# Where DVE sums two of an even job's three cache pages beside gated linear attention

## The chip, the cores and the metric

One core of a Trainium2 chip runs the whole program. The metric is the device time of one execution in microseconds. Engines: PE (TensorE, with PEld for its weight loads), DVE (VectorE), ACT (ScalarE), POOL (GpSimd) and SP (SyncE, which only issues DMAs here). Each engine runs its own instructions strictly in the order in which they are written; engines meet through counting semaphores (`S("name")`).

## What is computed

One inference step of a small hybrid decoder: a gated-linear-attention (GLA) layer, then a stick-breaking attention layer over a shared, paged K/V cache, for 512 prompt tokens and for 8 sample tokens with 2048 cached positions each. What matters here:

```
# GLA, per head h of 4, in 8 chunks of 64 tokens
o_intra = tril(q_in @ k_in^T) @ v
S_c     = decay_c * S_(c-1) + k_dec_c^T @ v_c        # state steps, chunk by chunk
o       = o_intra + q_in @ S_(c-1)
out     = (rms_norm(o) * silu(g)) @ w_out             # g = hn @ w_in[:, gates]

# scores of the 8 samples against the cache: 8 x 16 pages of 128 keys, 16 heads of 64
z[page, key, head] = sum_d k_cache[page, key, head, d] * q[sample, head, d]
```

The scores of the cache don't depend on the prompt's GLA. They are spread over the long run of matrix products as filler for POOL, DVE and ACT.

## The kernel before, in words

**Jobs.** The prompt's matrix products are cut in jobs of 128 output columns (`PHASES`, L38): gk 0 and 1, q 2 to 5, k 6 to 9, v 10 to 17, g 18 to 25, wo0 26 to 33, ple0 34 to 41, q1 42 to 49, g1 50 to 57 and so on. A job up to g uses three products of split weights (`product`, L1727): ACT makes the high part of the weights (`split_hi`, L736), DVE the low part (`split_lo`, L1210 to L1216), and PE waits for it by `w_split`. Jobs of wo0, ple0, q1 and g1 are unsplit (L1744, L1747).

**The page pipeline.** The cache's keys come as 128 pages of 512 KB. For page n: SP loads it in a slot (`load_page`, L533 to L542); POOL, or for some pages DVE (L1401), multiplies it by the sample's query (`multiply_pages`, L634 to L642); then DVE sums over each head's 64 features (`score_pages`, L1389 to L1403, the TENSOR_REDUCE of L1402), or ACT for some pages with 16 activations (`sum_page`, L900 to L909). `PAGES_AT` (L66 to L74) deals pages to jobs, and job j sums the pages dealt to job j-1: in phase g three a job. With `FEW` = 32, pages 0 to 31 turn round in four slots (L84 to L94) and later ones in eight, so in phase g page n is loaded when page n-4 has been summed (`slot_free`, L498 to L512, semaphore `k_used`). SP issues in order: pages, the rows of queries (L544 to L550), and ahead of page 36 `w_up0`, which waits for the last attention output (`o_mm`) and the last store of states (`st_out`, L563 to L567). From page 32 on the first page of each job is summed by ACT (`ACT_SUMS`), in wo0 to ple0. Page n+8 then waits for it.

**Phase g on PE** (L2041 to L2053 and L1984 to L2039). Job 18+u is a gate product; u//2 is the head h. An even u is followed by `gla_turned(h-2)` (transposes, L2037), `gla_output(h-1)` (L2022, L2026), which waits for all 8 state steps of head h-1, and `gla_scores(h)` (transposes L1995, products L2003), which from h = 2 waits for `gated`, that is for `gate_o(h-2)` on DVE. An odd u is followed by `gla_states(h)` (L2015), the products that the state steps take in. After job 25 come products of wo0 mixed with `gla_turned(2)`, `gla_output(3)` and `gla_turned(3)` (L2061 to L2077).

**Phase g on DVE** (L1463 to L1490). The order is written out by hand. Each job: `gate_normed` (L1453) on the product; an odd job then has the 8 state steps of its head (`state_steps`, L1435 and L1438), an even one `gate_o(h-2)` (L1447); then `gate_silu` (L1459), which waits for ACT's sigmoid; an even job also the masked copy of the scores (L1481). `state_steps(h)` of a head after the first waits until the previous head's final state has been stored from the same tile (`st_out`; the store is ACT's, L928) and its outputs are done (`o_mm`). `score_pages(job, part, parts)` sums a part of a job's pages. With three pages, (0, 2) is the first page and (1, 2) the other two. The calls before the change:

- an odd job u (up to 5), at its end: the first page of its three
- the next even job, between norm and silu: the other two pages of the odd job
- an even job, at its end: all three of its pages (two in job 18)

**Phase g on ACT** (L946 to L973): high splits, sigmoid of the gate (L788), for an even job the store of the state, the sum of squares and copies of the output (`o_copies`, L926 to L934), the copy of the keys (L970) and the norm of the output (`o_rms`, L936 to L944).

**wo0.** On DVE each job adds the residual (`add_residual`, L1497) and sums pages; on ACT (L996 to L1007) each job asks for weights, sums its first page, and then copies and squares the residual tile (`x_hi`, L747, and L761). The first product of ple0 takes in those eight tiles.

Of the kernel before, what the change touches and what calls it, by code (L numbers as in the profile page):

```python
# [152 lines left out]
def pages_at(job):  # L153
    return range(PAGES_THROUGH.get(job - 1, 0), PAGES_THROUGH.get(job, NPAGES))
# [17 lines left out]
def on_pool(n):  # L172

    return all(n - pages_at(j)[0] < pool_share(j) for j in PAGES_THROUGH if n in pages_at(j))


def pool_pages(n):

    return sum(on_pool(i) for i in range(n))


def on_act(n):

    return any(n in pages_at(j)[:ACT_SUMS.get(j, 0)] for j in PAGES_THROUGH)
# [11 lines left out]
def banks_of(j):  # L196

    m = tiles_through(j) - 1
    if wide(j):
        return (2 * (m % 2), 2 * (m % 2) + 1)  # L200
    return (m % 4,) if m >= FOUR_BANKS else (m % 2,)
# [31 lines left out]
def build(nc, x_prompt, x_sample, state_gla, cache_k, cache_v, page_table, p_prompt, p_sample,  # L233
# [3 lines left out]
    with ExitStack() as ctx:  # L237
# [179 lines left out]
        def S(name):  # L417
            if name not in sems:
                sems[name] = ctx.enter_context(nc.semaphore(name))
            return sems[name]  # L420
# [166 lines left out]
        def _(pool):  # L587
# [90 lines left out]
            def cut_causal(h):  # L678

                A = psig[h % 2]  # L680
                for e, (_, _, blocks) in enumerate(ZBANKS):
                    pool.wait_ge(S("sig_p"), h * len(ZBANKS) + e + 1)
                    if len(blocks) == 2:
                        own_blocks = A[:, 2 * P:4 * P].rearrange("p (b n) -> p b n", n=P)
                        pattern = [[0, 2], [-1, P]]
                    else:
                        c = PSEG[blocks[0]] + blocks[0] * P
                        own_blocks, pattern = A[:, c:c + P], [[-1, P]]
                    ins = nc.gpsimd.affine_select(out=own_blocks, in_=own_blocks, compare_op=ALU.is_ge, fill=0.0, base=-1,
                                                  pattern=pattern, channel_multiplier=1)  # L690
                ins.then_inc(S("sig_cut"), 1)
# [515 lines left out]
        def _(dve):  # L1207
            own = Steps(dve, S("dve_steps"))

            def split_lo(j):  # L1210

                if j >= NJOBS or unsplit(j):
                    return
                dve.wait_ge(S("w_hi"), splits_through(j))
                raw, hi, lo = split_views(j)
                nc.vector.tensor_tensor(lo, raw, hi.bitcast(F32), ALU.subtract).then_inc(S("w_split"), 1)  # L1216
# [172 lines left out]
            def score_pages(job, part=0, parts=1):  # L1389

                pages = pages_at(job - 1)
                for n in pages[len(pages) * part // parts:len(pages) * (part + 1) // parts]:
                    if on_act(n):
                        continue
                    at, b = slot[SLOT_OF[NSB + n]][:], n // NPG
                    if on_pool(n):
                        dve.wait_ge(S("k_mul_pool"), pool_pages(n + 1))
                    else:
                        dve.wait_ge(S(f"qb_in{b % 2}"), 16 * (b // 2 + 1))
                        dve.wait_ge(S(f"slot_in{SLOT_OF[NSB + n]}"), 16 * SLOT_TURN[NSB + n])  # L1400
                        own.then(nc.vector.tensor_tensor(at, at, qb[:, b % 2, :], ALU.mult))  # L1401
                    nc.vector.tensor_reduce(zall[:, n % NPG, b * SH:(b + 1) * SH], at.rearrange("p (h d) -> p h d", d=HD),  # L1402
                                            AX.X, ALU.add).then_inc(S("k_used"), 1)  # L1403

            for u in range(1, 8):
                j = PHASES["v"][0] + u
# [18 lines left out]
            def state_steps(h, chunks):  # L1425

                if h and chunks[0] == 0:
                    dve.wait_ge(S("st_out"), 16 * h)
                    dve.wait_ge(S("o_mm"), h)
                for c in chunks:  # L1430
                    kv = chunk_bank(c)
                    if c % 4 == 0:
                        dve.wait_ge(S("kv_mm"), h * NCH + c + 4)
                    if c == 0:
                        ins = nc.vector.tensor_copy(states[:, 0, :], kv)  # L1435
                    else:
                        dve.wait_ge(S("st_step"), h * NCH + c)
                        ins = nc.vector.scalar_tensor_tensor(states[:, c, :], states[:, c - 1, :],  # L1438
                                                             dec[:, h, c:c + 1], kv, ALU.mult, ALU.add)
                    ins.then_inc(S("st_step"), 1)  # L1440

            def gate_o(h):

                dve.wait_ge(S("o_t"), h + 1)
                for vt in range(2):
                    g = gT[:, 2 * h + vt, :]
                    last = nc.vector.tensor_tensor(g, bank[(4 if h < GH - 1 else 6) + vt], g, ALU.mult)  # L1447
                last.then_inc(S("gated"), 1)

            def gate_normed(j):  # L1450

                src, like = product_of(j)
                nc.vector.tensor_tensor(src, src, like(rstd[:]), ALU.mult).then_inc(S("g_n"), 1)  # L1453

            def gate_silu(j, u):

                src = bank[banks_of(j)[0]]
                dve.wait_ge(S("sigm"), u + 1)
                nc.vector.tensor_tensor(gT[:, u, :], src, work[:, 2 + u % 2, 0:NP_TOK], ALU.mult).then_inc(S("evac"), 1)  # L1459
# [3 lines left out]
            for u in range(8):  # L1463
                h = u // 2
                j = PHASES["g"][0] + u
                if u % 2 == 0 and u:
                    split_lo(j + 1)
                gate_normed(j)
                if u % 2:
                    state_steps(h, range(NCH))  # L1470
                    gate_silu(j, u)
                    if h < GH - 1:
                        score_pages(j, 0, 2)
                else:
                    if h >= 2:
                        gate_o(h - 2)
                    if h:
                        score_pages(j - 1, 1, 2)
                    gate_silu(j, u)
                    dve.wait_ge(S("att_mm"), h + 1)  # L1480
                    nc.vector.copy_predicated(attT[:, h % 2, :].rearrange("p (b n) -> p b n", b=TB), attm,  # L1481
                                              bank[5].rearrange("p (b n) -> p b n", b=TB)).then_inc(S("att_out"), 1)
                    split_lo(j + 2)
                    score_pages(j)

            score_pages(PHASES["g"][0] + 7, 0, 2)
            gate_o(GH - 2)
# [34 lines left out]
            for u in range(8):  # L1522
                j = PHASES["wo0"][0] + u
# [3 lines left out]
            for u in range(8):  # L1527
                j = PHASES["ple0"][0] + u
# [7 lines left out]
            for u in range(8):  # L1536
                j = PHASES["q1"][0] + u
# [27 lines left out]
            for i in range(24):  # L1565
                u = i % 8
                j = PHASES["g1"][0] + i
# [85 lines left out]
            for u in range(8):  # L1653
                j = PHASES["wo1"][0] + u
# [13 lines left out]
            for u in range(8):  # L1668
                j = PHASES["ple1"][0] + u
# [22 lines left out]
        def _(pe):  # L1692
# [34 lines left out]
            def product(j, x0, wait_x=False, tiles=range(KT)):  # L1727
# [8 lines left out]
                if unsplit(j):  # L1736
# [12 lines left out]
                    if tiles[-1] == KT - 1:  # L1749
                        last.then_inc(S("mm"), 1)  # L1750
                    return
                _, wh, wl = split_views(j)
                for k in range(KT):
                    if wait_x:
# [383 lines left out]
            def scores(h):  # L2138

                i = h // 2  # L2140
                if h == 0:
                    pe.wait_ge(S("evac"), last_tile("V"))
                pe.wait_ge(S("q_low"), h + 1)
                pe.wait_ge(S("qz_zero"), min(h + 1, 4))
                for e, (bk, _, blocks) in enumerate(ZBANKS):
                    if bk == SHARED and h >= 2:
                        pe.wait_ge(S("at_shared"), h - 1)
                    if h:
                        pe.wait_ge(S("sig_p"), (h - 1) * len(ZBANKS) + e + 1)
                    for q in blocks:  # L2150
                        c0, n = ZB[q][1], (q + 1) * P
                        for low in range(2):
                            last = nc.tensor.matmul(bank[bk][:, c0:c0 + n], qz[h % 4][:, low, q * P:(q + 1) * P],
                                                    (KE, KO)[h % 2][:, i, 0:n], start=(low == 0), stop=(low == 1),
                                                    skip_group_check=True)
                    last.then_inc(S("z_p"), 1)
# [149 lines left out]
```

## Time and profile before

| what | value |
|---|---|
| median of 3 runs | 868.82 us (868.79 to 869.54) |
| the profiled execution, its own time | 872.96 us |
| its span, first to last instruction | 871.2 us |
| PE busy | 818.4 us (94%) |
| DVE busy | 563.7 us (65%) |
| ACT busy | 480.7 us (55%) |
| POOL busy | 344.9 us (40%) |
| DMA | 236.79 MB, mean 272 GB/s |
| mean granted TensorE clock | 0.992 |

The span is that of one profiled execution; the times of the runs are taken without a profile. Phase g takes some 165 to 241 us of the span, wo0 some 243 to 318, ple0 and q1 from there to 437, and g1 follows. In a timeline, the number ahead of a bracket is the duration, and the bracket tells how long the engine was idle before that instruction and what ended the idle time ("issue": nothing that the profile shows). PE's products show two records for each matmul in 32-bit floats.

### The profile page before, as it was taken

The page shows a single profiled execution, that of the slowest core. Times are in us where ns is not written, and L with a number is a line of the kernel's source. Part 1 is how long each engine was busy: PE and PEld are TensorE (multiplying, and loading weights), DVE is VectorE, ACT ScalarE, POOL GpSimd, SP SyncE. Part 2 cuts the span into 40 slices and gives each one's busy share as a digit, 9 for nine tenths or more (in the row PEclk, how much of TensorE's full clock was granted, in tenths as well). Part 3 has the DMA queues.
Part 4 walks back from the last instruction along what each step waited for, and adds up shares of the span by engine and source line. Part 5 has one row for each costly group of instructions (what it writes and reads, how often), then busy time and mean ns, then how long its engine had stood idle before and what let it go on. Part 6 is the DMA issues. An engine that isn't in the chain of part 4 may idle for free.

```text
span 871.2 us, 14850 instructions
## 1 busy us (share of the span) xinstructions
PE 818.4 (94%) x5001; PEld 572.5 (66%) x5001; DVE 563.7 (65%) x620; ACT 480.7 (55%) x1603; POOL 344.9 (40%) x211
## 2 busy tenths in 40 slices
PE   5999999998999999999999999999969998999995
PEld 3666667876754434444488878777745454899995
DVE  4545375798966677878997744331179996655553
ACT  4611382335666677769886433412288895444433
POOL 3000000866685997885894000000266663011110
PEclk9999999999999999999999999999999999999998
DMA  9999868655689997997997099998888989521202
GB/s 330 380 368 340 315 221 297 209 187 212 206 283 378 385 344 250 328 350 262 392 392 272 1 351 335 361 331 290 314 317 299 341 332 370 184 97 49 98 1 99
DMA packets 109820, 236.79 MB, mean 272 GB/s; under 512 B 7505, under 2 KB 66712, under 8 KB 109488
## 3 DMA queue, kind: packets, MB, share of 16 engines
q1 hardware_dynamic: 51136, 174.29, 54.8%
q10 hardware_dynamic: 58608, 61.54, 21.0%
q8 instruction: 40, 0.66, 0.3%
q14 instruction: 36, 0.29, 0.1%
HBM read 222.54 MB, written 13.27 MB: 271 GB/s over the span
## 4 chain that ended last, share of the span: by engine, by line
PE 61%; DMA 12%; DVE 10%; ACT 8%; issue 3%; POOL 3%; SPq 2%; ACTq 0%; DVEq 0%; POOLq 0%
PE ps L1760 17%; PE ps L1747 13%; PE ps L1763 8%; PE ps L2197 5%; PE ps L1744 4%; DMA slot<-in_cache_k_dram 4%; PE ps L1724 2%; DMA work<-in_cache_v_dram 2%; DMA slot<-in_cache_v_dram 2%; POOL slot L641 2%; DVE w_lo L1216 2%; DMA w_raw<-in_gla_w_in_dram 2%; ACT slot L907 2%; DVE states L1438 2%; DVE zall L1402 1%
## 5 line engine op out<-in xcount | busy, mean ns | idle before, releaser
L641 POOL TENSOR_TENSOR slot<-slot,qb 128x1024 f32<-128x1024 f32 x97 | 249.2, 2600 | 100.2 <-DMA slot<-in_cache_k_dram 62.8
L1402 DVE TENSOR_REDUCE zall<-slot 128x16 f32<-128x1024 f32 x97 | 116.9, 1215 | 25.3 <-POOL slot L641 24.2
L1216 DVE TENSOR_TENSOR w_lo<-w_raw,w_hi 128x1024 fp32r<-128x1024 f32 x57 | 80.9, 1419 | 80.1 <-ACT w_hi L736 80.0
L907 ACT ACTIVATE slot<-slot 128x64 f32<-128x64 f32 x496 | 118.6, 241 | 18.4 <-POOL slot L641 18.3
L736 ACT CAST w_hi<-w_raw 128x1024 fp32r<-128x1024 f32 x58 | 60.6, 1045 | 72.1 <-PE ps L1763 36.3
L907 ACT ACTIVATION_READ_ACCUMULATOR slot<-slot 128x1 f32 x496 | 92.9, 187 | 0.0
L1747 PE MATMUL ps<-xn,w_raw 128*128 128x512 f32 x192 | 85.1, 595 | 1.3 <-ACT xn L747 1.3
L1747 PE MATMUL ps<-xn,w_unsplit 128*128 128x512 f32 x192 | 83.7, 593 | 0.0
L1763 PE MATMUL ps<-xa_hi,w_hi 128*128 128x512 f32 x200 | 81.7, 409 | 0.1
L1760 PE MATMUL ps<-xb_hi,w_hi 128*128 128x260 f32 x384 | 78.9, 287 | 1.1 <-DVE w_lo L1216 0.9
L1763 PE MATMUL ps<-xa_hi,w_lo 128*128 128x512 f32 x200 | 79.1, 396 | 0.0
L1763 PE MATMUL ps<-xa_lo,w_hi 128*128 128x512 f32 x200 | 78.7, 393 | 0.0
L1760 PE MATMUL ps<-xb_lo,w_hi 128*128 128x260 f32 x384 | 77.1, 282 | 0.0
L1760 PE MATMUL ps<-xb_hi,w_lo 128*128 128x260 f32 x368 | 74.0, 282 | 0.0
L2197 PE MATMUL ps<-slot,zs 128*32 128x512 f32 x480 | 63.1, 609 | 7.7 <-DMA work<-in_cache_v_dram 3.2
L1747 PEld LDWEIGHTS ps<-xn,w_unsplit 128*128 128x128 f32 x192 | 36.3, 190 | 46.2 <-issue 46.2
L1747 PEld LDWEIGHTS ps<-xn,w_raw 128*128 128x128 f32 x192 | 35.8, 190 | 46.6 <-issue 44.2
L1239 DVE TENSOR_TENSOR work<-ps,rstd 128x520 f32<-128x520 f32 (+1 forms) x40 | 27.7, 694 | 58.7 <-PE ps L1760 37.6
L1401 DVE TENSOR_TENSOR slot<-slot,qb 128x1024 f32<-128x1024 f32 x31 | 61.2, 1973 | 0.0
L1760 PEld LDWEIGHTS ps<-xb_hi,w_hi 128*128 128x128 f32 x384 | 59.0, 189 | 2.5 <-DVE w_lo L1216 1.1
L1760 PEld LDWEIGHTS ps<-xb_lo,w_hi 128*128 128x128 f32 x384 | 59.1, 188 | 0.0
L1760 PEld LDWEIGHTS ps<-xb_hi,w_lo 128*128 128x128 f32 x368 | 56.7, 188 | 0.0
(326 smaller groups left out, 1506.3 us busy)
## 6 DMA issues: line engine op xcount, KB each, us to landing
slot<-in_cache_k_dram SPq DMA_DIRECT2D x128, 512.0 KB, 6.2
slot<-in_cache_v_dram SPq DMA_DIRECT2D x120, 512.0 KB, 5.8
w_raw<-in_gla_w_in_dram ACTq DMA_DIRECT2D x12, 1024.0 KB, 6.6
slot<-in_gla_w_in_dram SPq DMA_DIRECT2D x24, 512.0 KB, 9.2
w_raw<-in_w_kv_dram ACTq DMA_DIRECT2D x8, 1024.0 KB, 11.0
w_raw<-in_w_ple_gate_dram ACTq DMA_DIRECT2D x6, 1024.0 KB, 5.5
s<-in_state_gla_dram SPq DMA_DIRECT2D x1, 4096.0 KB, 22.4
out_dram<-s ACTq DMA_DIRECT2D x4, 1024.0 KB, 8.2
```

What stands on the lines that cost most here:

```text
L641: nc.gpsimd.tensor_tensor(slot[s][:], slot[s][:], qb[:, (n // NPG) % 2, :], ALU.mult).then_inc(S("k_mul_pool"), 1)
L736: nc.scalar.copy(hi, raw).then_inc(S("w_hi"), 1)
L907: ins = nc.scalar.activation(part, part, ACT.Copy, accum_out=zall[:, n % NPG, b * SH + h:b * SH + h + 1])
L1216: nc.vector.tensor_tensor(lo, raw, hi.bitcast(F32), ALU.subtract).then_inc(S("w_split"), 1)
L1239: nc.vector.tensor_tensor(like(dst), src, like(rstd[:]), ALU.mult).then_inc(S("evac"), 1)
L1401: own.then(nc.vector.tensor_tensor(at, at, qb[:, b % 2, :], ALU.mult))
L1402: nc.vector.tensor_reduce(zall[:, n % NPG, b * SH:(b + 1) * SH], at.rearrange("p (h d) -> p h d", d=HD), AX.X, ALU.add).then_inc(S("k_used ...
L1744: last = nc.tensor.matmul(pp[m % 2][:, t, 0:H2], w[:, k, :], x[:, t * H2:(t + 1) * H2], start=(k == 0), stop=(k == KT - 1))
L1747: last = nc.tensor.matmul(bank[banks_of(j)[0]], w[:, k, :], x[:, 0:NP_TOK], start=(k == 0), stop=(k == KT - 1))
L1760: last = nc.tensor.matmul(pp[m % 2][:, t, 0:H2], w[:, k, :], x[:, t * H2:(t + 1) * H2], start=(k == 0 and first), stop=(k == KT - 1 and w ...
L1763: last = nc.tensor.matmul(bank[banks_of(j)[0]], w[:, k, :], x[:, 0:NP_TOK], start=(k == 0 and first), stop=(k == KT - 1 and w is wl))
L2197: last = nc.tensor.matmul(pp[3][32 * g:32 * g + 32, t, :], zs[:, c:c + 32], slot[SLOT_OF[e0 + g]][:, t * 512:(t + 1) * 512], start=(j0 == ...
```

## The change

On an odd job of phase g the two later pages of the even job before it are summed, in one more call behind the state steps and the gate; the even job sums at its end only the first page (one of its two pages in job 18, one of three in 20, 22 and 24). The order of pages stays 0, 1, 2 and so on. Nothing else differs: PE, ACT, POOL and SP have the same instructions.

```diff
                 if u % 2:
                     state_steps(h, range(NCH))
                     gate_silu(j, u)
+                    score_pages(j - 1, 1, 2)
                     if h < GH - 1:
                         score_pages(j, 0, 2)
                 else:
...
                     nc.vector.copy_predicated(attT[:, h % 2, :].rearrange("p (b n) -> p b n", b=TB), attm,
                                               bank[5].rearrange("p (b n) -> p b n", b=TB)).then_inc(S("att_out"), 1)
                     split_lo(j + 2)
-                    score_pages(j)
+                    score_pages(j, 0, 2)
 
             score_pages(PHASES["g"][0] + 7, 0, 2)
             gate_o(GH - 2)
```

## Rows read from the trace of the kernel before

**Rows 1.** The page, chain that ended last, share of the span by engine
```profile
PE 61%; DMA 12%; DVE 10%; ACT 8%; issue 3%; POOL 3%; SPq 2%; ACTq 0%; DVEq 0%; POOLq 0%
```

**Rows 2.** Windows: us, busy us (and count) by engine, clock, DMA share, GB/s
```profile
176.00:241.00 65.00, 58.87 (x317) 45.14 (x316) 58.02 (x70) 33.57 (x71) 43.16 (x19) 1.00 0.59 197
260.00:265.00 5.00, 5.00 (x19) 2.73 (x18) 0.46 (x1) 0.00 (x0) 5.00 (x3) 1.00 0.87 306
265.00:270.00 5.00, 4.49 (x11) 1.81 (x10) 1.52 (x3) 1.89 (x3) 2.42 (x2) 1.00 1.02 411
262.00:318.00 56.00, 54.71 (x139) 23.75 (x138) 40.65 (x35) 38.42 (x244) 45.84 (x19) 1.00 1.03 383
318.00:472.00 154.00, 154.00 (x470) 82.33 (x471) 129.94 (x112) 121.30 (x809) 121.06 (x46) 1.00 0.91 327
```

**Rows 3.** Timeline of PE: start us, us, line, operation, tiles, [idle before it <-releaser]
```profile
186.70 1.99 PE L2022 MATMUL ps<-vtok,attT 128*128 128x256 f32 x8 [1.01 <-DVE states L1438]
...
207.34 0.41 PE L2037 MATMUL ps<-ident,qT 128*128 128x128 f32 x2 [2.00 <-DVE states L1438]
...
213.64 0.63 PE L1995 MATMUL ps<-ident,kT 128*128 128x128 f32 x4 [1.64 <-issue]
...
234.31 0.63 PE L1995 MATMUL ps<-ident,kT 128*128 128x128 f32 x4 [1.37 <-issue]
...
247.59 0.41 PE L2037 MATMUL ps<-ident,qT 128*128 128x128 f32 x2 [0.54 <-DVE states L1438]
...
317.87 1.13 PE L1747 MATMUL ps<-xn,w_raw 128*128 128x512 f32 x2 [0.78 <-ACT xn L747]
```

**Rows 4.** Timeline of DVE, same columns
```profile
201.37 1.22 DVE L1402 TENSOR_REDUCE zall<-slot 128x16 f32<-128x1024 f32 x1 [3.40 <-POOL slot L641]
...
216.94 1.22 DVE L1216 TENSOR_TENSOR w_lo<-w_raw,w_hi 128x1024 fp32r<-128x1024 f32 x1
...
221.98 1.22 DVE L1402 TENSOR_REDUCE zall<-slot 128x16 f32<-128x1024 f32 x1 [1.56 <-POOL slot L641]
...
224.16 3.65 DVE L1438 SCALAR_TENSOR_TENSOR states<-states,dec,ps 128x256 f32<-128x256 f32 x7
...
229.45 2.96 DVE L1216 TENSOR_TENSOR w_lo<-w_raw,w_hi 128x1024 fp32r<-128x1024 f32 x1
...
232.93 1.27 DVE L1447 TENSOR_TENSOR gT<-ps,gT 128x512 f32<-128x512 f32 x2
```

**Rows 5.** The chain in order of time: start us, us, what
```profile
313.27 3.93 ACT slot L907 x32
```

**Rows 6.** All page sums of DVE in 176 to 260: duration ns min/median/max
```profile
L1402 DVE TENSOR_REDUCE zall<-slot x26: 1202/1211/1226, 179.7 to 258.4; 128x16 f32<-128x1024 f32 x26
```

**Rows 7.** Timeline of POOL, same columns
```profile
219.56 11.77 POOL L641 TENSOR_TENSOR slot<-slot,qb 128x1024 f32<-128x1024 f32 x5 [4.59 <-DMA slot<-in_cache_k_dram]
...
282.10 6.98 POOL L641 TENSOR_TENSOR slot<-slot,qb 128x1024 f32<-128x1024 f32 x3 [7.25 <-DMA slot<-in_cache_k_dram]
...
289.41 41.99 POOL L641 TENSOR_TENSOR slot<-slot,qb 128x1024 f32<-128x1024 f32 x16 [0.33 <-DMA slot<-in_cache_k_dram]
```

**Rows 8.** DMA issues, median us to landing: 196 to 236, 185 to 200, 274 to 300
```profile
slot<-in_cache_k_dram SPq DMA_DIRECT2D x11, 512.0 KB, 4.4
...
out_dram<-states ACTq DMA_DIRECT2D x1, 128.0 KB, 7.9
...
slot<-in_cache_k_dram SPq DMA_DIRECT2D x15, 512.0 KB, 7.6
```

**Rows 9.** Page 48: load, time to landing, and multiplication (second of the two)
```profile
L542 SPq DMA_DIRECT2D slot<-in_cache_k_dram x1: 338/338/338, 288.6 to 288.6; - x1
...
DMA to landing us min/median/max: 6.8/6.8/6.8
...
L641 POOL TENSOR_TENSOR slot<-slot,qb x2: 2367/2368/2368, 295.0 to 297.3; 128x1024 f32<-128x1024 f32 x2
```

## The prediction, made before the changed kernel was run

> **What bounds the kernel now.** I read the chain of waits first: TensorE (PE) carries 61% of it, DMA, DVE and ACT most of the rest [rows 1]. Then the stages [rows 2]. In the linear-attention stretch, 176 to 241 us, PE is not full and the DMA engines are little more than half busy. From 262 to 318 PE has 54.71 of 56 us and the DMA share is 1.03. From 318 to 472 PE is busy for all of 154 us, so what PE has gained at 318 it keeps there.
>
> PE's timeline has five stalls in the stretch [rows 3]: 1.01, 2.00 and 0.54 us for the state steps (L1438), and 1.64 and 1.37 us ahead of L1995, put down to "issue". The code tells those two: gla_scores waits for gate_o, whose L1447 ends on DVE at 234.20 [rows 4], just before PE goes on at 234.31. Together 6.56 us, the most that a quicker attention can give. At 317.87 PE waits 0.78 us for ACT's last copy of a residual tile [rows 3], which stands behind an ACT page sum that began as POOL's multiplication ended [rows 5], and that goes back to a page load. So the page pipeline and PE finish this stage together: a gain of PE alone buys nothing there.
>
> **What is late on DVE.** Before odd job 23, DVE idles 1.56 us for POOL's third page, sums it at 221.98, only then norms, and does the state steps from 224.16 (the copy before them from 223.7) to 227.8 [rows 4]. The change puts one sum there and two behind the gate. Seven sums move (one of two in job 18, two of three in 20, 22 and 24); none is added, none changes its engine, and the order of pages on DVE stays, so every counted wait keeps its meaning. A sum lasts 1.21 us [rows 6], and 1.12 us from start to start.
>
> **Part by part**, pair by pair:
> - Job 19: one sum less ahead, so norm and steps come 1.12 us earlier and the stall of 1.01 us goes. DVE has no less work and meets job 20 about when it does now, but page 11 is loaded 5 us later, so POOL should be idle at split_lo(21). A low split takes 1.22 us beside an idle POOL (216.94), 2.96 us when a multiplication is running (229.45: it ends 1.08 us after POOL's, at 231.33) [rows 4, 7]. I take 1 us of help.
> - Job 21: before it three sums and 3.40 us of waiting [rows 4] become one sum: norm at about 198.0 (now 202.5). A new wait comes: the steps write over states, and the previous head's store (ACT, about 190.7) takes 7.9 us to land [rows 8]. So steps start at about 198.6 and end at 202.7 (now 207.2). PE wants them at 207.34-2.00-1.01 = 204.3: the 2.00 us stall goes. Behind the steps come silu, three sums (to 206.7), split_lo(23), norm, and gate_o(0) at 209.7. PE is there at 213.64-1.64-3.01 = 209.0 and waits 0.8 instead of 1.64. Gained so far: 3.85.
> - Job 23: steps end near 223.1 (now 227.8). PE is at the next scores at 234.31-1.37-3.85 = 229.1, so at L2037 4.66 us before (as 212.00 follows 207.34), 224.4: no stall. gate_o(1) at 230.0: about 1.0 us. Gained: 4.2.
> - Job 25: PE's product ends at about 237.1, DVE is there first; steps end at 242.3. PE wants them at 247.59-0.54-4.2 = 242.85: no stall. Sum: **4.7 us** at the last L2037. Bounds: 3.6 if both gate_o stalls stay whole (1.01+2.00+0.54), 6.56 if all five go.
>
> Behind the two moved sums stand DVE's next low split, norm and gate_o. Their cover is the time won before them; if POOL is late they hold the gate_o that PE waits for.
>
> **The page ring.** In this stretch there are four slots: page n is loaded once page n-4 is summed. A load lands in 4.4 us (median), POOL takes 2.35 (11.77/5) [rows 7, 8]. The moved sums hold back loads 11, 16, 17, 20 and 21 by 2 to 6 us. Page 16: load at 204.6, multiplied by 211.5, wanted by DVE at 210.8, a wait of 0.7. Followed page by page, the later ones are wanted about when ready, since jobs 22 to 25 come earlier too. Pages 28 to 31 then run back to back on POOL, and page 31 is summed at 259.6, where it is now. So the ring costs nothing by its end and wins nothing: pages 32 to 39, the w_up load and the query rows on SP's queue stay. SP is held by those sums alone; its other work here is behind them and not due.
>
> **The next stage takes part of it back.** Load 40 waits for ACT's sum of page 32, which waits for PE's first residual tile, so it moves by 4.7 us. POOL now idles 7.25 us before page 40 [rows 7], room for that. But the DMA share is 1.03 [rows 2], page loads take 7.6 us [rows 8], and the same bytes must move in less time. Lower bound: no page lands earlier than now. Page 48 lands at 295.4 and is multiplied at 297.3 [rows 9]; POOL runs without a gap from 289.41 [rows 7], so its chain, ACT's sum and PE's 317.87 can still come 1.9 us earlier. Upper: all 4.7. Two 1 MB weight loads asked for 4.7 us sooner meet a share of 0.87 in 260 to 265 [rows 2] and fill 0.7 us of it. And 383 GB/s over the stage against 411 in its best 5 us leaves up to 56*(1-383/411) = 3.8 us. The DMA row, full, is what this stage is nearest to, so I stay in the lower half: 1.9+0.7, and 0.6 for the rate, **3.2 us**. PE then has 1.5 us of new stall before 318. Nothing later moves: PE has no gap to 472, and the page sums up to there follow it.
>
> Sum on the profiled execution: 872.96 (its span of 871.2 and 1.8 around it) becomes 869.8. The runs' median is 868.82, 4.1 below it; the same step gives 865.6. 0.2%, 1.74 us, is about what a measurement can tell from no change.
>
> **Two rules weighed.** The 26 sums take 1.202 to 1.226 us, POOL busy or not [rows 6]. The Trainium skill (Advanced Engine Details and Errata, VectorE Performance Modes) says that the second Vector SBUF port is shared with GpSimd and that the two then block each other. By that, if the sums used that port too, each would wait for POOL like the low split, and the moved ones would cost gate_o over 1 us each; the rows deny it for the sums. Second, the stage from 262 to 318 moved 383 GB/s [rows 2]. The skill (DMA: Bandwidth & Descriptors, Specifications) gives about 358 GB/s of HBM for a core. By that the stage had no room and the third case below would be the forecast; the measured rate is above it already.
>
> **Rivals.**
> - All of it passes (gain 4.7 to 6.6, 864.1): page loads land as early as they are asked for. For it: page 48 has 1.9 us in hand, and the rate has been 411. Against: share 1.03.
> - The page stage swallows it (gain 0 to 1.7, 868.3): the attention gains, but weights asked for earlier delay pages 36 to 40, POOL's gapless run starts no sooner and PE waits some 4 us at the end of the stage. For it: the tie at 317.87 and the share. Against: POOL's 7.25 us idle, and the 1.9.
> - Slower, by the page ring: each moved sum returns its slot late. With landings of 8.9 us (4.4 twice over), page 16 is ready 4.5 us later, DVE waits for it ahead of silu(22), and the delay goes round every fourth page. It decides once page 38 is multiplied later than POOL's idle covers, 7.25 us, and 1.7 more to be seen: 8.9 late. Twice round gives 9.0, three times with shorter ones some 9.3: 2 us slower, 870.8. Against: nothing in 196 to 236 lands that slowly at the median [rows 8].
>
> **Chances.** Forecast (gain 1.7 to 4.7) 0.57, all passes 0.16, swallowed 0.20, ring slower 0.07. Faster by over 0.2%: 0.57+0.16 = 0.73; within: 0.20; slower: 0.07. The range takes in the forecast's bounds, most of the case where all passes (to 863.3, a gain of 5.5) and the upper part of the swallowed one (to 868.4).
>
> **What would show it.** On DVE the norms of jobs 19, 21, 23 and 25 at about 180.8, 198, 218 and 237; before the steps of job 21 a short wait for no engine (the store). On PE no stall for L1438, two short ones before L1995, the last L2037 pair of turns starting near 242.9 for head 2. Pages 28 to 31 on POOL where they are now. Load 40 near 270, POOL's gapless run from about 286, PE's last stall before 318 at about 314.7 and longer than 0.78. If L2037 for head 2 is not before 244, the first step is wrong; if it is, and PE reaches its gapless run only at 317, the second.

## The result, and the profile after

The changed kernel is **slower**: 876.37 us at the median of 15 runs (871.24 to 879.77), against 869.98 for the kernel before on the same chips (15 runs, 867.71 to 874.57). The ratio is 1.006, 95% interval 1.0047 to 1.0073. The prediction was 865.6, in a range from 863.3 to 868.4. Its three sign chances put 0.07 on this side.

The profiled execution of the changed kernel took 872.79 us (span 871.1), near its fastest run, and that of before 872.96, near the slow end of its runs. Those two pages, side by side, show no difference in the total; five more traces, told below, show where the 5 to 6 us go. The chain by engine, on the page of the changed kernel:

```profile
PE 71%; DMA 9%; DVE 7%; ACT 7%; issue 2%; SPq 1%; POOL 1%; ACTq 0%; DVEq 0%; POOLq 0%
```

Windows that answer to three of [rows 2], in the columns given there:

```profile
176.00:241.00 65.00, 62.33 (x338) 47.34 (x337) 57.44 (x74) 36.33 (x75) 45.59 (x20) 1.00 0.62 209
262.00:318.00 56.00, 51.80 (x119) 22.12 (x119) 43.07 (x34) 38.58 (x244) 51.16 (x20) 0.94 1.04 392
318.00:472.00 154.00, 154.00 (x467) 81.50 (x466) 125.55 (x110) 120.92 (x808) 119.58 (x45) 1.00 0.88 319
```

In this trace the attention has gained nearly what it should: PE is busy for 62.33 of 65 us, before 58.87 [rows 2]. But from 262 to 318 it is busy for 51.80 us where it had 54.71, at a granted clock of 0.94 where it had 1.00, while the DMA engines move more bytes than before (392 GB/s against 383). The new loss is in the stage whose page loads the prediction looked at. DVE's timeline of the changed kernel, in the columns of [rows 3] (from here on a line of before L1472 keeps its number, a later one is one higher):

```profile
180.97 0.68 DVE L1453 TENSOR_TENSOR ps<-ps,rstd 128x512 f32<-128x512 f32 x1
...
188.43 1.21 DVE L1216 TENSOR_TENSOR w_lo<-w_raw,w_hi 128x1024 fp32r<-128x1024 f32 x1
...
196.68 0.70 DVE L1453 TENSOR_TENSOR ps<-ps,rstd 128x512 f32<-128x512 f32 x1 [0.61 <-PE ps L1764]
...
200.27 0.42 DVE L1435 COPY states<-ps 128x256 f32<-128x256 f32 x1 [2.89 <-DMA out_dram<-states]
...
214.69 3.40 DVE L1216 TENSOR_TENSOR w_lo<-w_raw,w_hi 128x1024 fp32r<-128x1024 f32 x1
...
219.14 0.68 DVE L1453 TENSOR_TENSOR ps<-ps,rstd 128x512 f32<-128x512 f32 x1
...
237.99 0.70 DVE L1453 TENSOR_TENSOR ps<-ps,rstd 128x512 f32<-128x512 f32 x1 [1.81 <-PE ps L1764]
```

The norms (L1453) of jobs 19, 21, 23 and 25 start at 180.97, 196.68, 219.14 and 237.99, forecast 180.8, 198, 218 and 237. The low split of 21 lasts 1.21 us beside an idle POOL, as forecast; that of 24 meets a running multiplication and lasts 3.40. New is the wait of 2.89 us ahead of the copy of job 21, for the store of the previous head's last state. PE's timeline:

```profile
204.52 0.41 PE L2038 MATMUL ps<-ident,qT 128*128 128x128 f32 x2 [0.17 <-DVE states L1438]
...
211.38 0.63 PE L1996 MATMUL ps<-ident,kT 128*128 128x128 f32 x4 [2.20 <-issue]
...
230.84 0.63 PE L1996 MATMUL ps<-ident,kT 128*128 128x128 f32 x4 [0.17 <-issue]
...
243.44 0.41 PE L2038 MATMUL ps<-ident,qT 128*128 128x128 f32 x2
...
278.53 23.93 PE L1748 MATMUL ps<-xn,w_unsplit 128*128 128x512 f32 x48 [3.70 <-DMA w_unsplit<-in_gla_w_out_dram]
```

All three stalls for L1438 of [rows 3] are gone but for 0.17 us. Of the two waits for gate_o (ahead of L1996) the second went from 1.37 to 0.17 us, while the first grew from 1.64 to 2.20. L2038 (before L2037) for head 2 starts at 243.44, before at 247.59: 4.15 us gained of the 4.7 forecast. Then, at 278.53, stands a stall that no row of before had: 3.70 us for weights. The chain in order of time (start us, us, what), changed kernel:

```profile
261.72 16.77 DMA w_unsplit<-in_gla_w_out_dram
```

And the DMA issues from 258 to 272.5 us (number, KB each, median us to landing), first the kernel before, then the changed one:

```profile
slot<-in_cache_k_dram SPq DMA_DIRECT2D x5, 512.0 KB, 6.5
w_unsplit<-in_gla_w_out_dram ACTq DMA_DIRECT2D x2, 1024.0 KB, 11.8
w_up<-in_w_ple_up_dram SPq DMA_DIRECT2D x1, 1024.0 KB, 6.2
```

```profile
slot<-in_cache_k_dram SPq DMA_DIRECT2D x8, 512.0 KB, 6.9
w_unsplit<-in_gla_w_out_dram ACTq DMA_DIRECT2D x2, 1024.0 KB, 21.3
w_up<-in_w_ple_up_dram SPq DMA_DIRECT2D x1, 1024.0 KB, 5.8
w_raw<-in_w_ple_gate_dram ACTq DMA_DIRECT2D x1, 1024.0 KB, 29.1
```

Before, the weights of jobs 30 and 31 are asked for at 265.9, land 10.5 us later at 276.4, and PE takes them at 278.82: 2.4 us in hand (1.2 in e10, another trace of the kernel before, where they took 11.7). With the attention 4.2 us shorter they are asked for at 261.72, between `w_up0` (260.7) and the loads of pages 36 to 39 (261.9 to 265.2), where they used to come behind all four, and pages 40 and 41 follow at 270.5 and 272.0, where page 40 came at 274.7. Eight page loads are issued in the stretch, before five. The pages land hardly later (6.9 us for 6.5). The weights, on ACT's queue, take 16.77 us in place of 10.5, and the next 1 MB 25.9 in place of 13.1. So they land 2.1 us later than before although they were asked for 4.2 us earlier.

The idle PE then loses its clock. Windows of the changed kernel:

```profile
270.00:275.00 5.00, 4.84 (x12) 1.85 (x10) 4.57 (x4) 2.76 (x11) 5.00 (x3) 1.00 1.03 380
275.00:280.00 5.00, 1.47 (x2) 0.84 (x3) 3.91 (x3) 4.93 (x35) 3.95 (x3) 0.79 1.04 405
280.00:285.00 5.00, 5.00 (x7) 1.91 (x6) 3.91 (x4) 4.89 (x34) 5.00 (x2) 0.53 1.06 384
285.00:290.00 5.00, 5.00 (x13) 2.23 (x12) 4.17 (x4) 0.00 (x0) 3.85 (x3) 1.00 1.03 392
```

The granted clock falls from 1.00 to 0.79 and 0.53 (from 278 to 284 us it is 0.50, the 1.2 GHz level), and the 48 records of the first stretch of w_unsplit take 23.93 us where 48 take 20.76 at full clock: 3.2 us more behind a stall of 3.7. The Trainium skill (TensorE: Matmul & The Clock Gate, "What's actually happening") says that an engine left idle goes back to half rate; experiment 3 (run e4) tests that here.

### The profile page after: what moved, and what is told of

It reads as the page before. It is cut to its first block, busy times and chain, and to the rows that moved or that the text cites. A ratio compares the mean times of both kernels' runs of the same rounds, so it can differ in the third digit from the quotient of the medians.

```text
span 871.1 us, 14850 instructions
## 1 busy us (share of the span) xinstructions
PE 819.7 (94%) x5001; PEld 574.0 (66%) x5001; DVE 562.9 (65%) x620; ACT 480.9 (55%) x1603; POOL 350.0 (40%) x211
## 4 chain that ended last, share of the span: by engine, by line
PE 71%; DMA 9%; DVE 7%; ACT 7%; issue 2%; SPq 1%; POOL 1%; ACTq 0%; DVEq 0%; POOLq 0%
PE ps L1761 19%; PE ps L1748 18%; PE ps L1764 10%; PE ps L2198 5%; PE ps L1745 4%; PE ps L1725 2%; DMA w_raw<-in_gla_w_in_dram 2%; DMA w_unsplit<-in_gla_w_out_dram 2%; PE ps L2154 2%; PE ps L1776 2%; DMA work<-in_cache_v_dram 2%; DVE w_lo L1216 1%; PE ps L2182 1%; PE ps L1851 1%; ACT psig L1071 1%
## 5 line engine op out<-in xcount | busy, mean ns | idle before, releaser
L641 POOL TENSOR_TENSOR slot<-slot,qb 128x1024 f32<-128x1024 f32 x97 | 253.8, 2645 | 97.9 <-DMA slot<-in_cache_k_dram 60.3
L1216 DVE TENSOR_TENSOR w_lo<-w_raw,w_hi 128x1024 fp32r<-128x1024 f32 x57 | 78.7, 1381 | 79.0 <-ACT w_hi L736 78.8
L1748 PE MATMUL ps<-xn,w_unsplit 128*128 128x512 f32 x192 | 86.9, 611 | 3.7 <-DMA w_unsplit<-in_gla_w_out_dram 3.7
## 6 DMA issues: line engine op xcount, KB each, us to landing
w_raw<-in_w_kv_dram ACTq DMA_DIRECT2D x8, 1024.0 KB, 11.1
```

The lines of the kernel that those rows point to most:

```text
L641: nc.gpsimd.tensor_tensor(slot[s][:], slot[s][:], qb[:, (n // NPG) % 2, :], ALU.mult).then_inc(S("k_mul_pool"), 1)
L1748: last = nc.tensor.matmul(bank[banks_of(j)[0]], w[:, k, :], x[:, 0:NP_TOK], start=(k == 0), stop=(k == KT - 1))
```

## The experiments

Two theories stood after the result. **A, weights:** the attention's gain is real and is lost at one place, where weights asked for beside pages land late, PE idles and its clock falls. **B, spread:** the gain is lost all over the page stage, as the full DMA queue must move the same bytes in less time (the "swallowed" rival). Later a third came in, **C, store:** the gain is not always there, because the store of the state lands later than in the first trace. Marks of PE that are used below: the turn of head 2 (last L2037), the first product of w_unsplit, and the transposes of zall behind the scores' banks (L2126 of before); what lies behind that mark takes 394 to 399 us to the end of the span, 397.0 at the mean of both kernels, and 394.7 and 394.3 in e1 and e4.

**1. The pair of weights asked for earlier (e1), and the same in the kernel before (e2).**

```diff
                 sum_page(PHASES["g"][0] + u)
+            load_pair(PHASES["wo0"][0] // 2 + 2)
             act.wait_ge(S("gated"), GH - 1)
...
-                if j == PHASES["wo0"][0]:
-                    load_pair(j // 2 + 2)
```

> The changed kernel, with the weight load for jobs 30 and 31 (1 MB, into w_unsplit) asked for by ACT at about 243.5 us, before it waits for gate_o(2), in place of 261.7. Theory A (the attention does gain 4 us, and PE then meets weights that land late because they are asked for together with pages 36 to 39 and w_up; the wait lets TensorE's clock fall): the load lands before 262, PE's 3.7 us wait at 274.8 and the low clock after it are gone, and the stage ends earlier, PE's last stall being ACT's again: gain against the kernel before 2.5 to 3.5 us, 867 us. Theory B (the page ring is late by the moved sums, and the weights are only a sign of it): pages still set the pace, the time stays within 1 us of the changed kernel's, 875 to 877.

> The kernel before with the same weight load asked for early, nothing else. Theory A: PE did not wait for it there (it landed 2.4 us ahead of need), so the time stays within 1.5 us of the kernel before, 868 to 871; the load is only earlier. Theory B: the same. A gain of over 2 us here would say that the early load is worth something by itself, and that e1's gain is not to be laid to the pair of the two.

Measured: e1 871.26 us, ratio 1.001 (0.9989 to 1.0032); e2 870.38, 0.9989 (0.9973 to 1.0006). The loss is undone in e1, which theory B did not allow, and e2 shows that the edit by itself is worth nothing. But the gain that theory A expected (867 us) is missing. Part of the reason stands ahead of the weights: DVE waits 5.64 us for the store in this trace, and the turn of head 2 is at 246.25, 0.6 us before its mean in the kernel before. The rest is new. The weights, asked for at 242.02, take 12.8 us and now seem to hold back the last pages of the ring (POOL idles 6.87 us for a page before 254.76); DVE's gate_o(3), behind the sums of those, comes late, and PE waits. DVE's and PE's timelines of e1:

```profile
257.14 1.22 DVE L1401 TENSOR_REDUCE zall<-slot 128x16 f32<-128x1024 f32 x1 [4.40 <-POOL slot L641]
...
267.40 13.73 PE L1747 MATMUL ps<-xn,w_raw 128*128 128x512 f32 x28 [2.52 <-ACT xn L747]
```

The contention went from one place to another.

**2. `w_up0` taken out of the crowd (e3).**

```diff
                     sp.wait_ge(S("st_out"), 16 * GH)
-                    sp.dma_start(w_up0[:, :, :], ...).then_inc(S("up_in"), 16)
                 load_page(n)
+                if n == FEW + 19:
+                    sp.dma_start(w_up0[:, :, :], ...).then_inc(S("up_in"), 16)
```

> The changed kernel, with the 1 MB load of w_up on SP's queue moved from ahead of page 36 to behind page 51, long before its use at 335 us. Theory A: 1 MB less beside the weights asked for at 261.7: they land some 2 to 4 us earlier, so the 3.7 us wait shrinks to 0 to 2 us and with it the low clock; 868 to 873 us. Theory B: pages 36 to 39 are asked for 1.2 us earlier, which buys about 1 us, 875.

Measured: 870.52 us, ratio 0.9993 (0.9966 to 1.0021). One megabyte less ahead of them, and the weights land in 13.1 us, at 276.8, as PE comes for them (276.81): no stall, full clock, and the time is that of the kernel before. What theory A names is enough for the loss. It also says that `w_up0`, and not the pages alone, held the weights back. (`w_up0` is now asked for at 292.7, takes 9.8 us, and PE first uses it at 305.58, not at 335 as the expectation had it: 3.1 us in hand.) It leaves open why no gain is left: the turn of head 2 is at 245.40, only 1.4 us before its mean place in the kernel before (246.83, over three traces), behind a wait of 5.60 us for the store.

**3. The wait filled (e4).** Five products of a tile of ones, into a bank that nobody reads, stand ahead of the first product of w_unsplit; nothing else is computed or left out.

```diff
             for u in range(3, 8):
+                if u == 4:
+                    pe.wait_ge(S("gated"), GH)
+                    for _ in range(5):
+                        nc.tensor.matmul(bank[6], ones[:], x_whole(KT)[:, 0:NP_TOK], start=True, stop=True)
                 product(wo + u, KT)
```

> The changed kernel with five extra products of 128x512 (4.3 us) on PE ahead of job 30, where it waits 3.7 us for weights; their result is not used. They cost nothing while PE waits anyway, up to 0.6 us. If the low clock behind the wait (0.50 to 0.66 for some 6 us, 48 records in 23.93 us, not 20.76) comes of PE's idling, it is gone and the time falls by 2.5 to 3 us, to about 873.5. If it doesn't hang on the idling, the clock is still low there and the time stays or rises by 0.6.

Measured: 873.29 us, ratio 1.0027 (1.0009 to 1.0046), 3.1 us below the changed kernel's median (2.9 by the ratios). PE's timeline and windows of e4:

```profile
276.97 4.45 PE L2083 MATMUL ps<-xn,ones 128*128 128x512 f32 x10
281.38 8.85 PE L1748 MATMUL ps<-xn,w_unsplit 128*128 128x512 f32 x20
```

```profile
275.00:280.00 5.00, 5.00 (x13) 2.13 (x13) 3.51 (x4) 2.67 (x23) 4.37 (x2) 1.00 1.04 382
280.00:285.00 5.00, 5.00 (x13) 2.06 (x12) 4.96 (x4) 4.97 (x35) 4.97 (x2) 1.00 1.04 381
```

PE is held as long (4.45 us of filler in place of an idle 3.70), and the kernel is quicker: with the clock at 1.00, 48 records from 281.38 take 20.87 us. From the first product of w_unsplit to the transposes of zall it is 192.8 us in e4, and 195.3 to 195.9 in four traces of the changed kernel. So of the loss at this place some 3 us is the clock and not the wait.

**4. The wait for the store put where it is needed (e5), both edits (e6), both in the kernel before (e7).** In the traces of e1, e3 and e4 the store took 11.1 to 12.6 us, not 9.4 as in the first trace, and DVE stood in front of eight steps for it. Only the eighth step writes the part that is being stored.

```diff
                 if h and chunks[0] == 0:
-                    dve.wait_ge(S("st_out"), 16 * h)
                     dve.wait_ge(S("o_mm"), h)
...
                         dve.wait_ge(S("st_step"), h * NCH + c)
+                        if h and c == NCH - 1:
+                            dve.wait_ge(S("st_out"), 16 * h)
```

> The changed kernel, with DVE's wait for the store of the previous head's state moved from ahead of a head's 8 state steps to ahead of the eighth, the only one that writes the tile being stored. Traces of the changed kernel show that wait in job 21: steps start 2.9 to 5.6 us later than they could, PE stalls 0 to 2.9 us for them, and in some of them the clock falls behind the stall. Theory A1 (the wait matters only for the attention; behind it PE meets the late weights all the same): attention ends 2 to 3 us earlier than in those runs, PE waits longer for weights at about 272 to 275 us, the time falls by no more than 2 us, 874 to 877. Theory A2 (the store's stall and its low clock are the greater part of the loss): 869 to 872. Rival B (page ring): no change.

> The changed kernel with both: the store's wait ahead of the eighth step, and w_up asked for behind page 51. Theory A: no store wait, and weights that land in time or nearly: PE's gain of 4 us comes through to the stage's end, where ACT's page sum limits it as forecast: 865 to 867.5. If it is not under 869, something else takes the gain.

> The kernel before with the same two edits and without the change. Its steps didn't wait for the store and its weights landed in time, so theory A gives 868.5 to 871.5, no difference from the kernel before; only what w_up's late load gives the page loads, up to 1 us. If it is as fast as e6, the moved sums have no part in e6's gain.

| | the moved sums in | ratio to before (95%) | median us |
|---|---|---|---|
| neither edit (the change) | yes | 1.006 (1.0047 to 1.0073) | 876.37 |
| `w_up0` late (e3) | yes | 0.9993 (0.9966 to 1.0021) | 870.52 |
| store waited for last (e5) | yes | 1.000 (0.9982 to 1.0017) | 870.51 |
| both (e6) | yes | **0.9948** (0.9932 to 0.9963) | **865.35** |
| both (e7) | no | 0.9999 (0.9983 to 1.0015) | 870.54 |

Each ratio is to the kernel before on the same chip; the medians come from several chips. Each edit alone brings back some 5 to 6 us, both bring 10 to 11, and without the moved sums they bring nothing. e5 came out where its theory A2 had it (869 to 872), but e3 brings back as much with the store's wait in place, so neither cause is the greater one: the two add up. DVE and PE of e5, then of e6:

```profile
201.42 0.48 DVE L1439 SCALAR_TENSOR_TENSOR states<-states,dec,ps 128x256 f32<-128x256 f32 x1 [0.59 <-DMA out_dram<-states]
...
276.19 14.38 PE L1749 MATMUL ps<-xn,w_unsplit 128*128 128x512 f32 x29 [3.70 <-DMA w_unsplit<-in_gla_w_out_dram]
```

```profile
202.41 0.48 DVE L1440 SCALAR_TENSOR_TENSOR states<-states,dec,ps 128x256 f32<-128x256 f32 x1 [0.60 <-DMA out_dram<-states]
...
312.87 1.13 PE L1750 MATMUL ps<-xn,w_raw 128*128 128x512 f32 x2 [1.06 <-ACT xn L748]
```

In both the store still takes 12 us, but one step waits 0.6 us for it instead of eight behind a wait of 2.9 to 5.6, and the turn of head 2 starts at 241.13 and 242.06. e5 keeps the stall for weights, of 3.70 us, and gives most of its gain back there: it is 5.7 us ahead of the mean of before at the turn, 1.9 at the first product of w_unsplit and 1.1 at the zall mark. e6 has neither: its weights take 13.1 us from 260.3 and PE is there at 273.44, as they land. PE's last short stall of this stage is at 312.87 where it was at 317.87 [rows 3]: 5.0 us earlier, and 4.2 earlier than the mean of three traces of before (317.08). The zall mark is at 467.58, before at 471.8. **e6 beats both kernels.** As its gain passes through a page stage that is as full as before (391 GB/s from 262 to 318 us), theory B is not needed for the loss.

**5. How steady the two kernels are (e8, e11, e12 of the changed one, e9, e10 of before).** No edit.

> The changed kernel once more, for a second trace of it. Theory A: steps of job 21 wait for the store by 3 us or more, PE waits for w_unsplit at about 275 us by 3 to 5 us, and TensorE's clock is low for some 5 us behind it; the time 874 to 878, its median, as against 872.8 of the first trace.

> The kernel before, one more trace. Theory A: everything that the change costs lies ahead of the transposes of the sample scores (L2126, at 472.56 us in the first trace); here they start at 471 to 472.6 us, and 396 to 399 us follow.

> The same kernel before, same expectation: 471 to 472.6 us, then 396 to 399 us.

> The changed kernel, one more trace. Theory A: the same mark (L2127) at 474.4 to 477 us, with the store's wait of 3 to 6 us in job 21, the weights' wait of some 3.7 us and low clock behind it; the part behind the mark as long as before the change, 396 to 399 us. If that part is longer too, by 1 us or more, something behind 472 us also costs time, and theory A is not the whole.

> The same changed kernel, same expectation: mark at 474.4 to 477 us, 396 to 399 us behind it.

Measured: 875.36, 877.25 and 876.91 us changed, 869.3 and 869.23 before. Marks in us from the span's start: two of PE's as above, the start of DVE's sum of page 31 (the last of the ring), the issues of `w_up0` (SP) and of the weights of jobs 30 and 31 (ACT), how long these took to land, and PE's first product of them:

| | turn of head 2 | sum of page 31 | `w_up0` asked | weights asked | landed after | first w_unsplit | zall |
|---|---|---|---|---|---|---|---|
| before, first profile | 247.59 | 258.38 | 260.21 | 265.87 | 10.5 | 278.82 | 472.56 |
| before, e9 | 246.19 | 257.46 | 259.30 | 264.47 | 10.5 | 277.42 | 471.07 |
| before, e10 | 246.72 | 257.64 | 259.48 | 265.00 | 11.7 | 277.94 | 471.67 |
| changed, first profile | 243.44 | 258.89 | 260.73 | 261.72 | 16.8 | 278.53 | 474.40 |
| changed, e8 | 245.55 | 261.04 | 262.88 | 263.83 | 16.7 | 280.55 | 476.25 |
| changed, e11 | 245.92 | 261.08 | 262.91 | 264.20 | 18.5 | 282.73 | 478.25 |
| changed, e12 | 245.45 | 261.54 | 263.38 | 264.00 | 19.0 | 283.03 | 478.37 |

By the means (three of before, four changed) the changed kernel is 1.7 us ahead at the turn of head 2, loses 4.9 us from there to the weights (31.2 us before, 36.1 after) and another 1.9 us to the zall mark (the slow clock, about 3, less the 0.78 us stall at 317.87 that is gone, and some tenths): 5.1 us behind, where the ratio gives 5.2 and the two medians lie 6.4 apart. e11 and e12 pass the zall mark 1.3 and 1.4 us later than expected (474.4 to 477), as their weights cost more than the 3.7 us expected.

The table shows a second thing. `w_up0` is asked for 1.8 us behind the start of page 31's sum in all seven: page 35's load waits for that sum, and `w_up0` and pages 36 to 39 stand behind it. At the mean that sum starts 2.8 us later in the changed kernel (260.6 for 257.8), though only 0.5 later in the first trace, while the weights are asked for 1.7 us earlier. So the two meet, 1.0 us apart where they were 5.4, and in e8, e11 and e12 more because SP's loads come late (3.4 us) than because the weights come early (1.1). With the store's wait in place the sum of page 31 is late in e3 and e4 too (260.66, 260.72); without it, in e5 and e6, it is not (256.15, 257.07). No run moved the end of the ring alone. DVE, SP and ACT of e9, then of e11:

```profile
257.46 1.22 DVE L1402 TENSOR_REDUCE zall<-slot 128x16 f32<-128x1024 f32 x1 [1.09 <-POOL slot L641]
...
259.30 0.39 SPq L567 DMA_DIRECT2D w_up<-in_w_ple_up_dram  x1
...
264.47 1.03 ACTq L720 DMA_DIRECT2D w_unsplit<-in_gla_w_out_dram  x2
```

```profile
261.08 1.22 DVE L1402 TENSOR_REDUCE zall<-slot 128x16 f32<-128x1024 f32 x1 [1.09 <-POOL slot L641]
...
262.91 0.39 SPq L567 DMA_DIRECT2D w_up<-in_w_ple_up_dram  x1
...
264.20 2.54 ACTq L720 DMA_DIRECT2D w_unsplit<-in_gla_w_out_dram  x2
```

e11 also shows the waits that the first trace had only in part, on DVE and PE, then in windows:

```profile
202.75 0.42 DVE L1435 COPY states<-ps 128x256 f32<-128x256 f32 x1 [5.35 <-DMA out_dram<-states]
...
207.01 0.66 PE L2038 MATMUL ps<-ident,qT 128*128 128x128 f32 x2 [2.63 <-DVE states L1438]
...
282.73 3.78 PE L1748 MATMUL ps<-xn,w_unsplit 128*128 128x512 f32 x4 [5.42 <-DMA w_unsplit<-in_gla_w_out_dram]
```

```profile
206.00:211.00 5.00, 3.99 (x16) 3.47 (x16) 4.96 (x7) 0.00 (x0) 0.00 (x0) 0.66 0.24 69
280.00:285.00 5.00, 2.27 (x3) 1.17 (x4) 4.17 (x4) 3.78 (x25) 3.44 (x2) 0.64 1.05 383
```

There the store costs 5.35 us on DVE and 2.63 on PE, and the clock falls to 0.66 behind it; the weights cost 5.42 and the clock again. For the store's landing, DMA issues from 185 to 202 us, of before, of the changed kernel's first trace, and of e11:

```profile
slot<-in_cache_k_dram SPq DMA_DIRECT2D x5, 512.0 KB, 4.5
w_raw<-in_gla_w_in_dram ACTq DMA_DIRECT2D x1, 1024.0 KB, 6.8
out_dram<-states ACTq DMA_DIRECT2D x1, 128.0 KB, 7.9
```

```profile
slot<-in_cache_k_dram SPq DMA_DIRECT2D x5, 512.0 KB, 5.1
w_raw<-in_gla_w_in_dram ACTq DMA_DIRECT2D x1, 1024.0 KB, 8.8
out_dram<-states ACTq DMA_DIRECT2D x1, 128.0 KB, 9.4
```

```profile
slot<-in_cache_k_dram SPq DMA_DIRECT2D x5, 512.0 KB, 6.7
w_raw<-in_gla_w_in_dram ACTq DMA_DIRECT2D x1, 1024.0 KB, 11.8
out_dram<-states ACTq DMA_DIRECT2D x1, 128.0 KB, 12.3
```

Pages, weights and store all land later, together. From 190 to 195 us the DMA share is 0.71 to 0.77 in the three traces of the kernel before and 0.85 to 0.97 in those with the moved sums: loads held back by these sums fall into the store's stretch. This goes with its longer landing, though not trace by trace (the changed kernel's first has a share of 0.91 and 9.4 us, e6 0.86 and 11.9, and e10, of before, 0.77 and 9.2). The store is asked for 0.45 us behind the 1 MB of w_raw on ACT's own queue, and in all fourteen traces it lands 0.2 to 1.7 us behind it, so that it may simply wait for what is ahead of it. No run held the pages away or changed that order, so the cause is argued, not shown, and why the first trace was quicker stays open.

## Why the prediction was wrong

- **The attention's gain, 4.7 us.** Mechanism right in the first trace: the norms came as forecast to within 1.3 us, the second gate_o wait went, and the stalls for L1438 left but for 0.17 us. In e8, e11 and e12 the stall of 2.00 us is still there, as 2.29, 2.63 and 2.47. The term that was mis-sized is the new wait for the store: "takes 7.9 us to land" was taken over from one row of before [rows 8], where it hid; the kernels with moved sums show 9.4 to 12.6. That made a wait of "about 198.6" for the steps into 200 to 203, and 4.7 us into 1.7 at the mean. With that wait gone (e5, e6) the gain is 5.7 and 4.8 us against the mean of before. The term sat behind a wait of DVE with eight steps queued behind it, although one needed it.
- **The test was too weak.** "If L2037 for head 2 is not before 244, the first step is wrong": the first trace gave 243.44 and said right; three more gave 245.5 to 245.9 and say wrong. That one trace came out near the forecast was luck.
- **The page ring: not neutral.** That "the ring costs nothing by its end" fits the first trace (page 31's sum at 258.89, before 258.38) and fails in the others (261.0 to 261.5): 2.8 us late at the mean. The step took the store's landing for short, and with it the time at which DVE reaches the moved sums. Without the store's wait (e5, e6) the ring is on time, and in e6 the stage's last stall moves by 4.2 to 5.0 us. Directly the lateness costs PE little: it waits 0.78 us behind gate_o(3) in e12, 0.51 in the other traces of both kernels. But it pushes `w_up0` and pages 36 to 39 into the landing of the weights.
- **"The next stage takes part of it back": here it failed, in kind.** The step costed page loads, found 1.9 to 4.7 us of room for them, and was near enough on that: pages land 0.4 to 0.7 us later in the first trace, and in e6 all of the gain passes, 4 to 5 us, more than the 3.2. But it let the weights "fill 0.7 us" of idle DMA. It didn't ask when each of the two lands and who needs it. The trace of before had it: asked at 265.9, landed at 276.4, used at 278.82. Asked and used both 4.2 us earlier, they may take 12.9 us at most, and the row says 10.5 for a place behind the pages. Beside `w_up0` and the pages they took 16.7 to 19.
- **What turned a smaller gain into a loss** was in no case of the prediction: a stall of 3.6 to 5.9 us, and 3 us more for the clock that it takes down. The "swallowed" rival named the same two parties and had it the wrong way round: "weights asked for earlier delay pages 36 to 40". `w_up0` and the pages delayed the weights. The slower rival, with its chance of 0.07, had a late ring right and its path wrong: it wanted pages 8.9 us late, beyond what POOL's idle time covers, and a ring 2.8 us late was enough, through the weights.
- **The two rules weighed.** That the sums don't wait for POOL held: a sum on DVE takes 1.21 us, moved or not. The figure of about 358 GB/s (the Trainium skill, DMA: Bandwidth & Descriptors, Specifications) would have made the stage one without room; it moved 383 GB/s before and 392 after, and the measurement decides.

## What to carry to other kernels

When a stage is made shorter, list every load that is issued at its end with its time of landing and its time of use, not the pages alone: the one with the least in hand sets whether the gain passes, and moving it into a busier stretch, or a burst on another queue towards it, lengthens it as well. Take the landing of a transfer from the stretch it will fall in, as a range from several traces, and put a wait on it in front of the one instruction that needs it. A stall of PE costs more than its length if the clock falls behind it, so a gain of 1 or 2 us that ends in one can be a loss.

## What the runs showed of the hardware that was not expected

- **Two queues don't share evenly.** With `w_up0` and the page loads (4 KB rows) on SP's queue just ahead and behind, a 1 MB load of weights on ACT's queue (1 KB rows) goes from 10.5 us to between 16.7 and 19, a third one asked for behind it to 29.1 in the first trace, while a page goes from 6.5 to 6.9. With `w_up0` out of the way the first takes 13.1 (e3, e6). From 262 to 272 us of the changed kernel's first trace SP's queue moved 3.30 MB in 886 packets and ACT's 0.64 MB in 622. The Trainium skill (DMA: Bandwidth & Descriptors, "Queues, rings and completion order") says that each DMA engine takes turns between queues by the packet. That this puts the queue with small packets at a disadvantage is an inference; the direction agrees, and no run here changed the row's size.
- **A small store is no quick one.** 128 KB took 6.7 to 9.2 us in the kernels that load pages there as before, 9.4 to 12.6 in those with the sums moved, each time landing just behind the 1 MB load asked for ahead of it on the same queue.
- **Filler pays.** 4.45 us of unused products on PE in place of 3.70 us idle made the kernel 3.1 us quicker. The clock stayed at 1.00, which accounts for 2.5 to 3.1 us in the traces.
